# Weight loads requested between stores instead of ahead of them, in a two-layer attention backbone in fp32

## The reference

```python
for i in range(2):
    shift, scale, gate = split(silu(c) @ mod_w[i] + mod_b[i], 3)
    h  = rms_norm(x,  norm_g[i]) * (1 + scale)   + shift     # latent tokens
    hc = rms_norm(xc, norm_g[i]) * (1 + scale_c) + shift_c   # context tokens
    # layer 0: gated attention over all tokens; layer 1: neighbourhood attention:
    q, k, v, g = split(h @ w_in, 4)                          # 16 heads of 64
    s = concat(q . k_window * 64**-0.5 + bias, q . k_ctx * 64**-0.5)
    o = softmax(s)_loc @ v_window + softmax(s)_ctx @ v_ctx
    y = (o * silu(g)) @ w_out
    x = x + gate * y
return rms_norm(x, final_g)
```

## Time and profile before

| | |
|---|---|
| median of three runs | 1712.47 us |
| time of the profiled execution | 1710.27 us |
| its span (first to last instruction) | 1708.5 us |
| PE busy | 1601.2 us, 94% of the span |
| DVE, ACT, POOL busy | 800.2, 783.3, 310.3 us |
| mean DMA busy share (queue q1) | 47.6% |

### The profile page before, as it was taken

The page is one execution under the profiler, slowest core; times in us unless marked ns, Lnnn a source line. Parts: engine busy times, 40 slices in busy tenths (PEclk is TensorE's granted clock), DMA queues, the critical chain, the costliest instruction groups (busy, mean ns, idle before and its releaser), DMA issues. The chain is left out here.

```text
span 1708.5 us, 26314 instructions
## 1 busy us (share of the span) xinstructions
PE 1601.2 (94%) x9936; PEld 1381.2 (81%) x9936; DVE 800.2 (47%) x1866; ACT 783.3 (46%) x1802; POOL 310.3 (18%) x331
## 2 busy tenths in 40 slices
PE   7789999998999999989999999999897889999997
PEld 3167778888888889978877788889896889888886
DVE  1622221212888888864341221132222777667773
ACT  4212122122777777755551221122113777777772
POOL 0101210100222211100020000000900333333331
PEclk9989999999999999999999999999998999999999
DMA  7445510423511155033227555667537987787772
GB/s 282 161 136 181 176 49 25 136 72 137 127 23 22 22 164 164 20 113 88 71 62 217 177 172 161 197 184 236 149 93 225 298 284 247 244 264 253 260 239 62
DMA packets 190977, 264.56 MB, mean 155 GB/s; under 512 B 33682, under 2 KB 149988, under 8 KB 186724
## 3 DMA queue, kind: packets, MB, share of 16 engines
q1 hardware_dynamic: 188548, 254.49, 47.6%
q10 hardware_dynamic: 2304, 8.39, 1.9%
HBM read 193.62 MB, written 85.05 MB: 163 GB/s over the span
## 5 line engine op out<-in xcount | busy, mean ns | idle before, releaser
L1501 PE MATMUL p<-h_hi,w_hi 128*128 128x512 f32 (+1 forms) x448 | 168.2, 376 | 7.7 <-ACT g_stage L1616 3.8
L1502 PE MATMUL p<-h_lo,w_hi 128*128 128x512 f32 (+1 forms) x448 | 167.6, 374 | 0.0
L1503 PE MATMUL p<-h_hi,w_lo 128*128 128x512 f32 (+1 forms) x448 | 167.5, 374 | 0.0
L600 PE MATMUL pp<-h_hi,w_hi 128*128 128x512 f32 (+1 forms) x432 | 157.2, 364 | 8.6 <-PEq L124 8.6
L602 PE MATMUL pp<-h_hi,w_lo 128*128 128x512 f32 (+1 forms) x432 | 154.1, 357 | 0.0
L601 PE MATMUL pp<-h_lo,w_hi 128*128 128x512 f32 (+1 forms) x432 | 154.0, 356 | 0.0
L2036 DVE CUSTOM_DVE_ANT_0 nprob<-nS,bias_sets 128x640 f32<-128x640 f32 x128 | 105.3, 823 | 99.4 <-PE nS L1896 61.7
L1109 ACT ACTIVATE prob<-S,nm,qk_inv 128x512 f32<-128x512 f32 (+1 forms) x208 | 146.4, 707 | 8.6 <-DVE nm L1045 8.6
L1977 ACT CAST npt_hi<-nTB 128x256 fp32r<-128x256 f32 (+1 forms) x256 | 100.2, 427 | 81.0 <-PE nTB L1907 80.2
L1063 DVE TENSOR_TENSOR ptlo<-TB,pthi 128x512 fp32r<-128x512 f32 (+1 forms) x192 | 114.8, 598 | 29.8 <-ACT pthi L1121 27.9
L1121 ACT CAST pthi<-TB 128x512 fp32r<-128x512 f32 (+1 forms) x192 | 99.3, 517 | 62.9 <-PE TB L990 62.8
(11 more groups left out here) (228 smaller groups left out, 4308.6 us busy)
## 6 DMA issues: line engine op xcount, KB each, us to landing
kq_scratch<-p_stage SPq DMA_DIRECT2D x128, 256.0 KB, 4.1
kq_strip<-kq_scratch SPq DMA_DIRECT2D x32, 1024.0 KB, 7.6
bias_sets<-bias_scratch SPq DMA_DIRECT2D x64, 384.0 KB, 8.0
v_strip<-v_scratch SPq DMA_DIRECT2D x128, 128.0 KB, 2.8
wmod<-in_mod_w SPq DMA_DIRECT2D x24, 512.0 KB, 4.6
wside<-in_mod_w SPq DMA_DIRECT2D x12, 1024.0 KB, 5.1
bias_scratch<-bias_wide_scratch SPq DMA_DIRECT2D x16, 768.0 KB, 11.4
w_raw<-in_na_w_in SPq DMA_DIRECT2D x11, 1024.0 KB, 8.0
```

The lines of the kernel that those rows point to most:

```text
L600: pe.matmul(acc, whi[:, k, ws], hi[:, k, a:a + width], start=(k == 0), stop=False)
L1501: pe.matmul(ps[:, bank, 0:width], whi[:, k, ws], hi[:, k, a:a + width], start=(k == 0), stop=False)
L1502: pe.matmul(ps[:, bank, 0:width], whi[:, k, ws], lo[:, k, a:a + width], start=False, stop=False)
L1503: last = pe.matmul(ps[:, bank, 0:width], wlo[:, k, ws], hi[:, k, a:a + width], start=False, stop=(k == KT - 1))
```

## The change

`last_weights` takes the number of one piece. Piece 0 keeps the wait for `mm2` and for the stores of `p_stage`. The eight pieces are requested behind value stores 1, 3, 5, ..., 15 instead of all ahead of store 0. Number, size, source and target of the DMAs are the same, and PE, DVE, ACT and POOL keep their instructions.

```diff
-                def last_weights():
-                    sp.wait_ge(mm2, NT)
-                    for i in range(3):
-                        sp.wait_ge(stored[i], stored_by(ITEMS + (i - ITEMS) % 3))
-                    for k in range(KT):
-                        sp.dma_start(w1_raw[:, k, :], w_out1[k * P:(k + 1) * P, :]).then_inc(w1l[k], 16)
+                def last_weights(k):
+                    if k == 0:
+                        sp.wait_ge(mm2, NT)
+                        for i in range(3):
+                            sp.wait_ge(stored[i], stored_by(ITEMS + (i - ITEMS) % 3))
+                    sp.dma_start(w1_raw[:, k, :], w_out1[k * P:(k + 1) * P, :]).then_inc(w1l[k], 16)
...
-                last_weights()
                 for u in range(VB * TT):
                     v_store(u)
+                    if u % 2 == 1 and u // 2 < KT:
+                        last_weights(u // 2)
```

## The result

The changed kernel takes 1706.66 us (median of 7 runs, 1701.84 to 1708.23) against 1713.92 us for the kernel before in the same comparison (7 runs, 1706.51 to 1720.63): ratio 0.9947, 95% interval 0.9925 to 0.9969. Compared once more it took 1708.02 us (11 runs) against 1713.33 (25 runs): ratio 0.9968, interval 0.9954 to 0.9982. The forecast was 1704.9 us, a ratio of 0.9956, inside both intervals. By the two ratios the gain is 9.1 and 5.5 us; the ends of their intervals are 12.9 and 3.1 us. The difference of the medians is 7.3 and 5.3 us.

What follows compares the result with a forecast made beforehand. PE, busy for 94% of the span, was taken as the bound. Removing its stop (4.84 us) and the slow matmuls behind it (2.69) gave -7.53 us, from 1712.47 to 1704.9 us; range 1702.0 to 1709.0.

Steps and rivals of the forecast that it cites:

- The stop goes: Value stage: PE's wait between tiles 8 and 9, behind the late value store 0, vanishes, saving 4.84 us.
- The slow matmuls go: Value stage from tile 9: 27 matmul steps at half clock after PE's idle time return to full pace, saving 2.69 us.
- No new stall from the loads between stores: Value stage: SP and the DMA engines keep up with PE when loads go out between stores; cost 0.
- POOL unharmed: POOL's work on the loaded pieces: loads arrive early enough, so it ends near 1241 us as before; cost 0.
- Sum of the stage: Value stage: idle time of 4.84 us and slow matmuls of 2.69 us both go, together 7.53 us.
- I take 0, with 2 us either way: Next block, after the value stage: where its clock returns to full may shift; change taken as 0, within 2 us.
- the forecast's own sign: Sign of being wrong: next block, from first matmul to span's end, longer than 401.6 us by more than 2 us.
- given back in the next block: Rival, 7%: the stop goes, but the slow stretch after the blocks meet grows as long again, costing 3.9 us: 1708.8.
- Its base: Starting time of the whole kernel before the change: the median of its runs, 1712.47 us.
- The slower rival: Rival, 2%: in the value stage each load ahead makes a store land after 12.4 us, PE starves, total 1722 us.

## Why the prediction was right

- **The stop goes (4.84 us) with its cause.** Right. Store 0 went out 7.6 us earlier, tile 3 was copied at 1188.21 (forecast of the landing: 1188.5), and the runs with four, six and eight loads ahead show how the stop grows with them.
- **The slow matmuls go (2.69 us).** Right in its mechanism, and shown apart from the first term: 2.78 us with the stop filled, 0.07 of them a slightly shorter stop. Its size is that of one execution: in the repeat of the kernel before it was 1.5 us.
- **No new stall from the loads between stores.** Right, though two prices were low: a load request took 0.59 us, not 0.47, and the two context stores' requests 1.89, not 0.97 us. The slowest store took 4.8 us where the sum had 2.4 + 1.4 = 3.8. The buffers' room swallowed all three.
- **POOL unharmed.** Right: its last piece ended at 1241.2 (forecast 1241.1).
- **Sum of the stage.** Forecast 7.53, measured 7.55 us between the two first profiles. That it meets to 0.02 us is partly luck, for the forecast took its terms from the very profile it is compared with; against the repeat of the kernel before it is 6.74. The next block's first matmul was forecast at 1299.4 and measured at 1299.04.
- **"I take 0, with 2 us either way" for the block behind.** The size of that band was wrong. That block varies from 399.2 to 411.5 us over the runs with its instructions unaltered. By the forecast's own sign, a next block longer by more than 2 us, it would have been wrong (407.0 against 401.6); the sign was a bad one, since the unaltered kernel before moved by 9.9 us itself. The rival "given back in the next block" seemed to have come true, but not by its mechanism: the slow stretch behind the meeting of the blocks was 9.4 us long, as before (9.6), and the other time at half clock lay further on; in the repeat of the kernel before that stretch was 14.6 us. For the medians the scatter evens out in part, which is why the forecast held; the range of 1702 to 1709 covered the median, but single runs went from 1701.84 to 1711.2.
- **Its base.** The median of three that the forecast started from, 1712.47, stood for a kernel whose runs go from 1706 to 1721; that it lay within 1.5 us of the later medians (1712.05 to 1713.92) was luck in part.
- **The slower rival** was far off: the worst landing was 4.8, not the 10.3 us from which it would have decided.

What the forecast did not see is how little of the change was needed: all eight loads in a burst behind the first two stores, or four of the eight ahead of them, give the same stage.

## What to carry to other kernels

Look at what a queue holds ahead of the first small store of a stage: here store 0 took 8.4, 9.8 and 12.2 us to land behind four, six and eight loads. It costs nothing until the buffers behind it are full, so count the tiles of room and move only what exceeds them. A stop of PE has to be priced with the half-clock stretch behind it, which added 2.7 us to a stop of 4.8 and 1.5 to one of 5.2, while one of 1.3 us brought none. Compare stages between two profiles, not spans: here the value stage took 115.14 or 115.15 us in every run without a stop or added matmuls, beside a later block that varied by 12 us by itself.

## What the runs showed of the hardware that was not expected

- A stop of 1.3 us left the granted clock at 1.00; stops of 4.7 and 5.0 us were followed by 0.50. In one execution of the kernel before the stop was followed by a slow stretch of 5.9 us, in another by one shorter by about half (0.69 already in 1207 to 1209).
- In the run with 28 unused matmuls the clock fell to 0.50 without a long idle time: PE had been busy for 1.81 and 1.72 of 3 us, and no gap was over 1.1 us.
- The last block's time at half clock ranged from 15.7 to 40.5 us for one and the same kernel.
- A store requested behind 4 MB of loads in its own queue had its first packet started 8.6 us later, after nearly all of theirs; with the loads in another engine's queue it was 3.8 us, and from then on both went side by side.
